# Three places moved in the order of work of a two-block transformer kernel: layer 0's decay, the heads' exponentials, the turned forget gate

## The chip, the cores and the metric

The kernel runs on one core of a Trainium2 chip. The core has a matmul engine (TensorE, PE in the rows; its weight loads are PEld), two engines for elementwise work (VectorE, DVE, and ScalarE, ACT), GpSimd (POOL, idle here), and SyncE (SP), which issues every transfer. The engines run side by side and meet at semaphores. The metric is the time of one execution on the device in microseconds (us), as the median of several runs.

## The reference, cut to what matters

256 tokens of width 1024 pass through two layers of a first block and one layer of a second block, all in float32.

```
first block, twice:
  u = rms_norm(x) @ w_in[l]          -> q, k, v, gates, rank-16 vector rb, memory query qm
  log_a = log_sigmoid(rb @ w_gate_up[l] + b_gate_up[l]) / 16          # "decay"
  oa = softmax attention, 8 heads of 64, causal, ALiBi ("moba")
  ob = gated linear attention, 4 heads, decays log_a ("gla")
  mk, mv = split(rms_norm(mem) @ w_mem_kv[l]); om = softmax(qm mk^T) mv, 4 heads ("mem")
  x  = x + concat(oa, ob, om, each gated) @ w_out[l]
second block, once:
  fg = lb + (1 - lb) * sigmoid(f);  k = 1 - fg;  logf = log(fg)        # "forget"
  o_a = linear attention with k and logf, 8 heads of 128 ("hg")
  o_b = causal softmax attention with low-rank q and kv, 8 heads ("mla")
  x  = x + (sigmoid(gate_a) * (o_a @ w_a) + sigmoid(gate_b) * (o_b @ w_b)) @ w_out
  x  = x + mixture of 64 experts, top group, top 2 in it (SwiGLU, width 512)
  out = rms_norm(x)
```

## The kernel before

**Pieces.** Every projection of the two blocks is cut along its 1024 inputs into eight pieces of 128 rows, most of them 512 columns wide. A piece of weights is first *split* into two fp32r numbers: ScalarE writes the high part `w_hi` (line 1604, a copy), VectorE the low part `w_lo` (line 2010, or 2018 where a gain is folded in). TensorE then does the *mult* of the piece, six matmuls of 512 columns (lines 1116 and 1119): high by high, high by low, low by high, for each of the two tiles of 128 tokens. There are six places for split pieces, and the split of a piece is recorded five pieces ahead of its mult.

**The order is written out by a planner.** `order_of_work` makes one list of steps (`mult`, `split`, `scores`, `exp`, `turn k`, ...), and every engine carries out its own share of each step in this one order. A step whose share on an engine waits holds up all that stands behind it on that engine. Between the pieces stand the steps of the attentions. Two things place them: generators (`attention`, `gla`, `hgrn`) that are advanced by a turn every second piece or so, and `after(n, fn)`, which calls `fn` when n more pieces have been recorded (`tick`, called after each mult). `chain` strings several such calls together.

**The steps that the change touches.** The name of a step is given with its lines in the profile.

- *decay*: TensorE multiplies `rbT` by the gate's weights (line 1159), which VectorE has copied out of the bank as part of *gb out* (line 2007). VectorE adds the bias (2018), ScalarE does Abs, Exp and Ln (*decay log*, line 1601), VectorE ends it. The result is first used by *gla decay*, more than fifteen pieces later. Both 2 KB scratch buffers `sq` are held from *decay* to *decay end*; the next that needs them is *heads sq* of the memory's keys, whose chain goes on by *heads sum*, *heads root*, *heads norm* to *turn k*, transposes on TensorE (line 1099).
- *scores*, *exp*, *turn p*, *values* of a head: TensorE makes the scores (line 1176 for the memory heads, 1183 for moba), VectorE takes the row maxima (2021; for moba and mla it first adds the mask), ScalarE the exponentials (1601), TensorE transposes them (1099), ScalarE copies them back (1604), TensorE multiplies by the values (1215), VectorE scales (2018). A memory head's scores stay in their PSUM bank until its exponential has read them. In each layer the scores of memory heads 1, 2 and 3 all go to one bank (ps3 in layer 0, ps1 in layer 1), before and after the change.
- *forget*, *forget log*, *turn f*: after the sigmoid on ScalarE, VectorE makes fg and k for a tile of tokens (2010 twice, 2015), ScalarE the logarithm (1601), TensorE transposes k (1099, four 128x128), ScalarE copies it (1604). The transposed k is first read when the hg units of that half start, more than ten pieces later.
- *hg scale* on VectorE (2010) and *hg products* on TensorE (1357 and 1359) for a head of the linear attention.

**The experts.** After the mixers come 64 experts of three 2 MB matrices each, in 9 slots. SyncE issues a load as soon as the slot's last reader is through. The first of these loads waits until all engines have passed the end of the gates stage, the next seven for pieces of the last projections.

Of the kernel before, what the change touches and what calls it, by code (L numbers as in the profile page):

```python
# [131 lines left out]
class Plan:  # L132
# [7 lines left out]
    def add(self, *step):  # L140
        self.steps.append(step)
# [6 lines left out]
    def put(self, *banks):  # L148
        self.pool.extend(b for b, _ in banks)
# [49 lines left out]
def order_of_work(uses):  # L199
    P = Plan()  # L200
    add, get, put = P.add, P.get, P.put
# [19 lines left out]
    def after(n, fn):  # L221

        later.append([n, fn])

    def chain(*parts):

        def go(i):
            if i < len(parts):
                def one():
                    if parts[i][1]() is False:  # L230
                        return False
                    go(i + 1)

                after(parts[i][0], one)

        go(0)
# [85 lines left out]

    def attention(a, n):

        for i in range(n + 3):
            while len(P.pool) < 2:
                yield
            if 2 <= i < n + 2:
                B = get()
                add("turn p", a, i - 2, B)  # L330
                put(B)
            if i >= 3:
                B = get()
                add("values", a, i - 3, B)
                put(B)
                done.add((a, i - 3))
            if i < n:
                B = get()
                add("scores", a, i, B)
                P.scores[a, i] = B  # L340
                put(B)
            if 1 <= i < n + 1:
                add("exp", a, i - 1)
            yield

    def stats(n, first=1):
# [88 lines left out]
    def layer(l):  # L435
# [3 lines left out]
        def projections():  # L439
# [4 lines left out]
            for q in ORDER[l]:  # L444
                bs = []
                if q == "gb":
# [9 lines left out]
                        put(B)  # L456
                        chain((1, step("decay log", l, sq)), (1, step("decay end", l, sq, buffers=sq)))

                    after(2, decay)
                elif q == "qkv":  # L460
                    yield from mult(("h", l), [(None, 0, 128, 0, 0), (None, 128, 128, 0, 256), (0, 256, 256, 1, 0),
                                               (1, 256, 256, 1, 256)], bs, there)
# [92 lines left out]
    def group(half):  # L555
# [3 lines left out]
        sq, nt = [P.take("sq") for _ in range(2)], {}  # L559
        add("f out", half, bs, sq)  # L560
        put(*bs)
        for t in range(2):
            def forget(t=t):
                if not P.left("nt"):
                    return False
                nt[t] = P.take("nt")
                add("forget", half, t, sq[t], nt[t])

            def turned(t=t):
                B = get()  # L570
                add("turn f", half, t, nt[t], B)
                put(B)
                P.give(nt[t])
                done.add(("kTd", half, t))

            chain((1 + t, forget), (1, step("forget log", half, t, sq[t], buffers=[sq[t]])), (1, turned))
        yield
        bs = []
        yield from mult(("h", 2), PAIR, bs, there)
# [2327 lines left out]
```

How the kernel before makes its waits and increments, by code:

```python
    def wait_ge(self, sem, value):  # L106
        if sem is not None and self.met.get(sem.name, 0) < value:
            self.met[sem.name] = value
            self.e.wait_ge(sem, value)
# [979 lines left out]
        def tensor(e):  # L1089
# [2 lines left out]
            def room(B):  # L1092
                b, n = B
                w.wait_ge(*ever("outA", b, n - 1))
                w.wait_ge(*ever("outV", b, n - 1))
# [1 line left out]
            def turns(B, src, n, names):  # L1097
                for j in range(n):
                    i = e.transpose(ps(B)[:, j * 128:j * 128 + 128], src[:, j * 128:j * 128 + 128], ident)
                i.then_inc(mark(pe_turn, ("in", *B), *names), 1)
            for kind, *s in plan.steps:
                if kind == "mult":
                    q, lhs, k, jobs, first, final = s
                    hi, lo, ready = operand(lhs, k)
                    wh, wl = RW[q % NRW]
                    w.wait_ge(*at("lo", q))
                    w.wait_ge(*at(*ready))
                    for j, (t, c0, n, B, o) in enumerate(jobs):
                        if first and o == 0:
# [11 lines left out]
                        if names:  # L1122
                            i.then_inc(mark(pe_mult, *names), 1)
                elif kind == "turn":
                    n, k2, B = s
                    src = turned(n, k2)[0]
                    w.wait_ge(s_id, 16)
                    if n == 0:
                        w.wait_ge(s_x[k2 // 4], 16)
                    elif n == "mem":
                        w.wait_ge(s_mem, 16)
                    elif n in (1, 2):
```

## Time and profile before

| | us |
|---|---|
| median of 3 runs | 1625.37 |
| lowest, highest | 1623.73, 1626.02 |
| the profiled execution | 1626.19 |
| its span | 1624.2 |
| TensorE busy | 1470.4 |
| VectorE busy | 621.1 |
| ScalarE busy | 502.9 |

Around the span lie 2.0 us (1626.19 less 1624.2). The span falls in two parts. Up to about 680 us the core does the mixers: TensorE is busy nearly all the time, the transfers about a third of it. From 700 us the experts run and the 16 DMA engines are busy without a break, at about 427 GB/s. Busy time of TensorE is to be read with care, since matmuls overlap and their ends are modelled: the start of the next matmul tells more than the end of the last. The clock that is granted to TensorE is the column PEclk of the tables by window, 1.00 for 2.4 GHz and 0.50 for 1.2 GHz.

### The profile page before, as it was taken

The page shows a single profiled execution, that of the slowest core. Times are in us where ns is not written, and L with a number is a line of the kernel's source. Part 1 is how long each engine was busy: PE and PEld are TensorE (multiplying, and loading weights), DVE is VectorE, ACT ScalarE, POOL GpSimd, SP SyncE. Part 2 cuts the span into 40 slices and gives each one's busy share as a digit, 9 for nine tenths or more (in the row PEclk, how much of TensorE's full clock was granted, in tenths as well). Part 3 has the DMA queues.
Part 4 walks back from the last instruction along what each step waited for, and adds up shares of the span by engine and source line. Part 5 has one row for each costly group of instructions (what it writes and reads, how often), then busy time and mean ns, then how long its engine had stood idle before and what let it go on. Part 6 is the DMA issues. An engine that isn't in the chain of part 4 may idle for free.

```text
span 1624.2 us, 22403 instructions
## 1 busy us (share of the span) xinstructions
PE 1470.4 (91%) x9481; PEld 895.7 (55%) x9481; DVE 621.1 (38%) x1368; ACT 502.9 (31%) x1086; POOL 0.2 (0%) x4
## 2 busy tenths in 40 slices
PE   7999999989999999899999888888888889888886
PEld 6867787778786788744444433343333434433332
DVE  5766666665745657632211211111112111211112
ACT  6666665665645665311111100110011001010102
POOL 0000000000000000000000000000000000000000
PEclk9999999999999999999999999999999999999999
DMA  7422352424324247899999999999999999999995
GB/s 271 165 104 104 108 186 85 155 104 133 124 82 156 85 175 253 353 408 426 427 426 428 427 427 427 428 427 427 426 429 426 427 427 428 427 427 427 428 426 210
DMA packets 72682, 496.53 MB, mean 306 GB/s; under 512 B 6240, under 2 KB 10624, under 8 KB 47616
## 3 DMA queue, kind: packets, MB, share of 16 engines
q1 hardware_dynamic: 72576, 495.03, 74.6%
q8 instruction: 77, 1.26, 0.3%
q14 instruction: 29, 0.24, 0.0%
HBM read 493.96 MB, written 1.05 MB: 305 GB/s over the span
## 4 chain that ended last, share of the span: by engine, by line
PE 43%; DMA 42%; DVE 8%; ACT 5%; issue 1%; SPq 0%; DVEq 0%; ACTq 0%
DMA arena<-in_expert_w 42%; PE ps L1119 18%; PE ps L1465 5%; PE ps L1472 3%; DVE arena L2010 3%; PE ps L1116 2%; PE ps L1486 2%; DVE w_lo L2010 2%; PE ps L1497 2%; ACT arena L1601 2%; ACT arena L1604 1%; ACT w_hi L1604 1%; PE ps L1215 1%; PE ps L1447 1%; DMA arena<-in_w_mem_kv 1%
## 5 line engine op out<-in xcount | busy, mean ns | idle before, releaser
L1465 PE MATMUL ps<-arena 128*32 128x512 f32 x2048 | 250.0, 607 | 94.6 <-DMA arena<-in_expert_w 94.6
L2007 DVE COPY arena<-ps 128x512 f32<-128x512 f32 (+2 forms) x203 | 114.9, 589 | 514.3 <-PE ps L1465 415.4
L1604 ACT ACTIVATE arena<-ps 128x512 f32<-128x512 f32 (+5 forms) x244 | 121.5, 500 | 548.5 <-PE ps L1486 285.7
L1472 PE MATMUL ps<-arena 128*128 128x512 f32 x512 | 255.3, 622 | 0.0
L2010 DVE TENSOR_TENSOR w_lo<-arena,w_hi 128x512 fp32r<-128x512 f32 (+2 forms) x304 | 200.5, 672 | 140.6 <-ACT w_hi L1604 139.4
L1604 ACT ACTIVATE w_hi<-arena 128x512 fp32r<-128x512 f32 (+2 forms) x320 | 194.0, 621 | 111.0 <-PE ps L1119 97.2
L1465 PEld LDWEIGHTS ps<-arena 128*32 128x32 f32 x2048 | 55.7, 110 | 239.1 <-DMA arena<-in_expert_w 150.4
L1119 PE MATMUL ps<-w_hi,hT_hi 128*128 128x512 f32 (+3 forms) x448 | 178.8, 399 | 4.9 <-ACT arena L1601 2.1
L1497 PEld LDWEIGHTS ps<-arena 128*128 128x128 f32 x1024 | 130.0, 192 | 86.1 <-issue 84.1
L1119 PE MATMUL ps<-w_hi,hT_lo 128*128 128x512 f32 (+3 forms) x448 | 168.8, 377 | 0.0
L1119 PE MATMUL ps<-w_lo,hT_hi 128*128 128x512 f32 (+3 forms) x448 | 168.3, 376 | 0.0
L1601 ACT ACTIVATE arena<-ps 128x128 f32<-128x128 f32 (+2 forms) x140 | 48.6, 372 | 340.6 <-PE ps L1497 319.5
L1472 PEld LDWEIGHTS ps<-arena 128*128 128x128 f32 x512 | 88.3, 192 | 118.3 <-issue 117.5
L1497 PE MATMUL ps<-arena 128*128 128x32 f32 x1024 | 132.3, 273 | 0.8 <-DVE arena L2007 0.5
L1486 PE MATMUL ps<-arena 128*32 128x512 f32 x1024 | 123.9, 601 | 0.4 <-DVE arena L2010 0.4
L2010 DVE TENSOR_TENSOR arena<-arena,ps 128x128 f32<-128x128 f32 (+1 forms) x84 | 32.9, 399 | 195.1 <-PE ps L1497 186.6
L1119 PEld LDWEIGHTS ps<-w_hi,hT_hi 128*128 128x128 f32 x448 | 85.8, 192 | 28.9 <-issue 9.5
L1119 PEld LDWEIGHTS ps<-w_hi,hT_lo 128*128 128x128 f32 x448 | 85.9, 192 | 15.0
L1119 PEld LDWEIGHTS ps<-w_lo,hT_hi 128*128 128x128 f32 x448 | 86.2, 192 | 12.8 <-issue 1.2
L2010 DVE TENSOR_TENSOR arena<-arena 128x512 f32<-128x512 f32 (+7 forms) x191 | 73.9, 405 | 13.1 <-ACT arena L1601 7.8
L1601 ACT ACTIVATE arena<-arena 128x128 f32<-128x128 f32 (+7 forms) x132 | 52.2, 399 | 74.4 <-DVE arena L2010 40.7
L1447 PE MATMUL ps<-OH,arena 128*128 128x256 f32 x224 | 62.3, 400 | 3.6 <-DVE arena L2007 3.6
(154 smaller groups left out, 1378.4 us busy)
## 6 DMA issues: line engine op xcount, KB each, us to landing
arena<-in_expert_w SPq DMA_DIRECT2D x191, 2048.0 KB, 41.5
arena<-in_w_in SPq DMA_DIRECT2D x24, 2048.0 KB, 7.8
arena<-in_w_out SPq DMA_DIRECT2D x6, 2048.0 KB, 7.9
arena<-in_w_mem_kv SPq DMA_DIRECT2D x2, 2048.0 KB, 11.9
arena<-in_w_branch_hgrn SPq DMA_DIRECT2D x2, 2048.0 KB, 7.7
arena<-in_w_branch_mla SPq DMA_DIRECT2D x2, 2048.0 KB, 7.8
arena<-in_w_in SPq DMA_DIRECT2D x2, 1536.0 KB, 6.5
arena<-in_mla_w_uq SPq DMA_DIRECT2D x2, 1152.0 KB, 5.5
```

The source lines that it names most:

```text
L1116: i = e.matmul(ps(B)[:, o:o + 256], wp[:, 0, c0:c0 + 128], hp, start=st, stop=en, skip_group_check=True)
L1119: i = e.matmul(ps(B)[:, o:o + n], hp[:, t * 128:t * 128 + 128], wp[:, 0, c0:c0 + n], start=st, stop=en, skip_group_check=True)
L1215: o = e.matmul(ps(B)[:, j * dv:j * dv + dv], T[:, c0 + kt * 128:c0 + kt * 128 + 128], val[:, kt, i * dv:i * dv + dv], start=kt == 0, stop= ...
L1447: i = e.matmul(B, xk[:, t, ks], hot.bitcast(F32), start=t == 0, stop=t == 1)
L1465: o = e.matmul(B[32 * j:32 * j + 32, :], Xs[:, k, q:q + 32], Wn[:, k, :], start=i == 0, stop=i == 1)
L1472: i = e.matmul(acc[t][h][:, :], CT[ex % 2][:, t * 128:t * 128 + 128], Ys[:, h * 512:h * 512 + 512], start=ex == 0, stop=ex == NE - 1)
L1486: i = e.matmul(B[32 * j:32 * j + 32, :], hid[ex % 2][:, 32 * j:32 * j + 32], W2[:, j, h * 512:h * 512 + 512], start=True, stop=True)
L1497: i = e.matmul(B6[:, 128 * h + 32 * j:128 * h + 32 * j + 32], (H1s, H3s)[h][:, j * 128:j * 128 + 128], c("S4"), start=True, stop=True)
L1601: return e.activation(o, i, f, scale=scale, **more)
L1604: return e.activation(o, i, ACTF.Copy, scale=scale)
L2007: return e.tensor_copy(o, i)
L2010: return e.tensor_tensor(o, a, b, op)
```

## The change

It moves steps in the planner's list; no instruction is added or dropped, and there are 31 loads of a function table on ScalarE in either program.

```diff
     def attention(a, n):
 
+        through = set()
+
+        def exp(i):
+            if i not in through:
+                through.add(i)
+                add("exp", a, i)
+
...
                 add("scores", a, i, B)
                 P.scores[a, i] = B
                 put(B)
+                after(1, lambda i=i: exp(i))
             if 1 <= i < n + 1:
-                add("exp", a, i - 1)
+                exp(i - 1)
             yield
...
-                    after(2, decay)
+                    after(5 if l == 0 else 2, decay)
...
-            chain((1 + t, forget), (1, step("forget log", half, t, sq[t], buffers=[sq[t]])), (1, turned))
+            chain((1 + t, forget), (1, step("forget log", half, t, sq[t], buffers=[sq[t]])), (3, turned))
```

1. Layer 0's *decay* stands after mult 12 instead of mult 9; its log and its end move with it.
2. The exponentials of head i stand behind the first mult after its scores, not behind the scores of head i + 1. The code is the same for all three softmax attentions, so it holds for the 8 memory heads of both layers, the 16 moba heads and the 8 mla heads.
3. *turn f* stands two mults later, for each of the two halves.

**ScalarE, memory heads 0 to 3 of layer 0.** `ps,arena 128x256 x2` is one head's exponential, `w_hi` a split, `128x16 x2` is *heads root* of the queries, `ps 128x512` alone the copy of turned exponentials, and `16x4x16` with the two rows behind it *gla collect*. Before:

```order
L1604 ACTIVATE w_hi_63<-arena 128x512
L1604 ACTIVATE w_hi_53<-arena 128x512
L1601 ACTIVATE arena<-arena 128x16 x2
L1601 ACTIVATE arena<-ps,arena 128x256 x2
L1604 ACTIVATE w_hi_55<-arena 128x512
L1604 ACTIVATE w_hi_57<-arena 128x512
L1604 ACTIVATE arena<-ps 128x512
L1601 ACTIVATE arena<-ps,arena 128x256 x2
L1604 ACTIVATE arena<-ps 16x4x16 x4
```

The same place of the changed kernel, whose line numbers are 8 higher:

```order
L1612 ACTIVATE w_hi_63<-arena 128x512
L1609 ACTIVATE arena<-ps,arena 128x256 x2
L1612 ACTIVATE w_hi_53<-arena 128x512
L1609 ACTIVATE arena<-arena 128x16 x2
L1612 ACTIVATE w_hi_55<-arena 128x512
L1609 ACTIVATE arena<-ps,arena 128x256 x2
L1612 ACTIVATE w_hi_57<-arena 128x512
L1612 ACTIVATE arena<-ps 128x512
L1612 ACTIVATE arena<-ps 16x4x16 x4
```

Head 0's exponential now stands ahead of a split and of *heads root*; head 1's ahead of a split and of the copy of head 0's turned exponentials. Further on, head 2's stands behind one split after *gla collect* instead of behind two splits and two copies.

**ScalarE, layer 0's decay log.** It is the row `arena<-arena 128x256 x3`; the row with the table load and the one behind it are *stats root* of the memory rows. Before:

```order
L1596 ACT_TABLE_LOAD
L1601 ACTIVATE arena<-arena 128x2 x2
L1604 ACTIVATE w_hi_57<-arena 128x512
L1604 ACTIVATE w_hi_59<-arena 128x512
L1601 ACTIVATE arena<-arena 128x256 x3
L1604 ACTIVATE w_hi_61<-arena 128x512
```

And in the changed kernel, up to *heads sq* of the memory's keys (the last two rows):

```order
L1604 ACT_TABLE_LOAD
L1609 ACTIVATE arena<-arena 128x2 x2
L1612 ACTIVATE w_hi_57<-arena 128x512
L1612 ACTIVATE w_hi_59<-arena 128x512
L1612 ACTIVATE w_hi_61<-arena 128x512
L1612 ACTIVATE w_hi_63<-arena 128x512
L1612 ACTIVATE w_hi_53<-arena 128x512
L1609 ACTIVATE arena<-arena 128x256 x3
L1612 ACTIVATE w_hi_55<-arena 128x512
L1612 ACTIVATE w_hi_57<-arena 128x512
L1612 ACTIVATE arena<-ps,arena 128x256 x2
L1609 ACTIVATE arena<-ps 128x256 x2
```

Three splits that stood behind the decay log now stand ahead of it, and two splits are left between it and *heads sq*.

**TensorE, the second half's turn f.** `arena 128x128 x4` is one *turn f*, `arena 128x128` alone the first matmul of *hg products* of the fourth head of that unit. Before, from the end of mult 211:

```order
L1119 MATMUL ps<-w_hi_55,hT_lo 128x512
L1099 MATMUL ps<-arena 128x128 x4
L1357 MATMUL ps<-arena 128x128
L1359 MATMUL ps<-arena 16x16 x4
L1359 MATMUL ps<-arena 32x32 x2
L1359 MATMUL ps<-arena 64x64
```

In the changed kernel, from the end of mult 211 to the first *turn f*, with mult 212 between:

```order
L1127 MATMUL ps<-w_hi_55,hT_lo 128x512
L1365 MATMUL ps<-arena 128x128
L1367 MATMUL ps<-arena 16x16 x4
L1367 MATMUL ps<-arena 32x32 x2
L1367 MATMUL ps<-arena 64x64
L1127 MATMUL ps<-w_hi_57,hT_hi 128x512
...
L1107 MATMUL ps<-arena 128x128 x4
```

The products no longer have the two *turn f* ahead of them (the other stood ahead of mult 211).

## Rows read from the trace of the kernel before

**Rows 1.** Page, part 1: busy time of the engines, share of the span, instructions.
```profile
PE 1470.4 (91%) x9481; PEld 895.7 (55%) x9481; DVE 621.1 (38%) x1368; ACT 502.9 (31%) x1086; POOL 0.2 (0%) x4
```

**Rows 2.** Page, part 4: the chain that ended last, by engine.
```profile
PE 43%; DMA 42%; DVE 8%; ACT 5%; issue 1%; SPq 0%; DVEq 0%; ACTq 0%
```

**Rows 3.** Windows: stretch, length, busy us (instructions) by engine, PEclk, DMA share, GB/s.
```profile
500.00:600.00 100.00, 99.07 (x480) 75.75 (x479) 56.94 (x123) 61.54 (x129) 0.00 (x0) 1.00 0.36 127
...
700.00:800.00 100.00, 97.08 (x713) 44.04 (x715) 22.48 (x50) 11.50 (x23) 0.00 (x0) 0.98 1.01 428
```

**Rows 4.** Timeline of SyncE: start, length, issues of expert loads.
```profile
644.44 83.79 SPq L2755 DMA_DIRECT2D arena<-in_expert_w  x17
```

**Rows 5.** Waits of TensorE, 0 to 620 us: total us, times, longest.
```profile
PE ps L1176 <- ACT arena L1601: 5.4, 4, 1.6
...
PE ps L1119 <- ACT arena L1601: 2.1, 3, 1.5
```

**Rows 6.** Windows around TensorE's stops, columns as in Rows 3.
```profile
29.80:36.00 6.20, 6.20 (x16) 4.91 (x17) 4.00 (x12) 4.51 (x9) 0.00 (x0) 0.50 0.08 8
...
114.00:117.60 3.60, 3.60 (x9) 2.24 (x10) 1.32 (x2) 1.11 (x2) 0.00 (x0) 0.58 0.00 0
...
362.30:367.00 4.70, 4.65 (x18) 3.56 (x19) 3.61 (x6) 3.46 (x7) 0.00 (x0) 0.65 0.15 21
...
431.00:435.00 4.00, 3.77 (x11) 3.00 (x11) 2.11 (x5) 3.84 (x7) 0.00 (x0) 0.63 0.00 0
...
133.00:142.00 9.00, 8.12 (x39) 5.89 (x39) 6.44 (x16) 6.44 (x16) 0.00 (x0) 1.00 0.35 144
```

**Rows 7.** Timeline: start, length, instruction, [idle before <-releaser]; decay (PE), split 14 (ACT).
```profile
29.78 1.22 PE L1159 MATMUL ps<-arena 16*128 16x128 f32 x4 [3.10 <-DVE arena L2007]
...
31.07 0.70 ACT L1604 ACTIVATE w_hi<-arena 128x512 fp32r<-128x512 f32 x1
```

**Rows 8.** Waits of ScalarE from 33 to 46 us.
```profile
ACT w_hi L1604 <- PE ps L1119: 3.1, 4, 1.2
```

**Rows 9.** Timeline: memory keys' root (ACT), norm (DVE), first turn k (PE).
```profile
45.43 0.46 ACT L1601 ACTIVATE arena<-arena 128x8 f32<-128x8 f32 x2 [1.40 <-DVE arena L2015]
...
48.01 0.76 DVE L2010 TENSOR_TENSOR arena<-ps,arena 128x256 f32<-128x256 f32 x2
...
49.76 0.38 PE L1099 MATMUL ps<-arena 128*128 128x128 f32 x2
```

**Rows 10.** Timeline of TensorE: scores of memory heads 2 and 3, layer 0.
```profile
104.94 1.13 PE L1176 MATMUL ps<-arena 64*128 64x256 f32 x4 [1.60 <-ACT arena L1601]
...
112.78 1.13 PE L1176 MATMUL ps<-arena 64*128 64x256 f32 x4 [1.11 <-ACT arena L1601]
```

**Rows 11.** Timeline of VectorE: maxima of head 1; gla collect's share.
```profile
101.46 0.69 DVE L2021 TENSOR_REDUCE arena<-ps 128x2 f32<-128x512 f32 x1
...
107.10 0.68 DVE L2010 TENSOR_TENSOR arena<-ps,arena 128x512 f32<-128x512 f32 x1
```

**Rows 12.** Timeline of ScalarE: head 1's exponential; gla collect; a moba split.
```profile
103.87 0.47 ACT L1601 ACTIVATE arena<-ps,arena 128x256 f32<-128x256 f32 x1
...
107.88 1.85 ACT L1604 ACTIVATE arena<-ps 16x64 f32<-16x64 f32 x7 [2.99 <-DVE arena L2010]
...
151.82 0.63 ACT L1604 ACTIVATE w_hi<-arena 128x512 fp32r<-128x512 f32 x1 [1.17 <-PE ps L1119]
```

**Rows 13.** Timeline: TensorE's first turn f, VectorE's second forget, first half.
```profile
362.35 0.66 PE L1099 MATMUL ps<-arena 128*128 128x128 f32 x4 [2.95 <-DVE arena L2015]
...
364.26 0.43 DVE L2015 TENSOR_SCALAR arena<-arena 128x512 f32<-128x512 f32 x1
```

**Rows 14.** Timeline, second half: VectorE's hg scale; TensorE's second turn f and products.
```profile
439.17 1.29 DVE L2010 TENSOR_TENSOR arena<-arena 128x512 f32<-128x512 f32 x2
...
439.31 0.66 PE L1099 MATMUL ps<-arena 128*128 128x128 f32 x4
440.61 0.46 PE L1357 MATMUL ps<-arena 128*128 128x128 f32 x2 [0.64 <-DVE arena L2010]
```

## The prediction, as it was put on record before the changed kernel ran

> **What bounds the kernel now.** I read the page first. TensorE is busy for 91% of the span [rows 1]. The chain that ended last is 43% TensorE and 42% transfers [rows 2]. The two do not compete for the same stretch: from 500 to 600 us TensorE is busy 99.07 of 100 us while the DMA share is 0.36, and from 700 to 800 us the DMA share is 1.01 at 428 GB/s [rows 3]. So the mixers are TensorE's and the experts are the transfers'. What joins them is the issue of expert loads: it starts at 644.44, and every load waits for TensorE or VectorE to free its slot [rows 4]. Behind that point nothing is changed. Each microsecond by which the mixers' last stage comes earlier should therefore shift the whole expert part rigidly, and each microsecond that TensorE does not lose before 640 us is one off the time. A step that is merely moved beside busy matmuls is worth nothing; what counts is where TensorE stops.
>
> I took the waits of TensorE next, then the windows around each stop. The memory heads' scores wait 5.4 us for exponentials, in four places [rows 5]. The first decay matmul waits 3.10 us [rows 7], the first turn f 2.95 us [rows 13]. A stop has a second price: after some of them the clock falls to 0.50 for a few us. The windows show means of 0.50, 0.58, 0.65 and 0.63 [rows 6]. What that costs is the stretch times one less the clock: 6.20 x 0.50 = 3.1 us behind the decay, 3.60 x 0.42 = 1.5 us behind memory head 3 (layer 1 has the same two stops and the same fall, so four score waits are two pairs), 4.70 x 0.35 = 1.6 us behind turn f, and 4.00 x 0.37 = 1.5 us at 431, behind a wait of 1.5 us that the change doesn't touch [rows 5]. But from 133 to 142 us the clock stays at 1.00 although TensorE is busy for only 8.12 of 9 us [rows 6]. A stop of about 1 us alone need not bring a fall.
>
> **Part 1, layer 0's decay.** Before, TensorE is through with mult 9 at 26.7 and stands until 29.78 for VectorE's copy of rb [rows 7]. Behind the move it goes straight into mults 10, 11 and 12, whose split pieces are ready, and comes to the decay at about 30.6, when the copy is done. So the wait of 3.10 and the slow stretch of 3.1 go: 6.2 us. What is late next? ScalarE. It is held by a table load and a root until 31.07 [rows 7] and then has to make the splits that TensorE uses from 32.6 on (mult 14). At 0.70 us on ScalarE [rows 7] and about as much on VectorE for a split, each low part is ready within 0.1 us of its mult up to mult 15. The decay log's three instructions (1.3 us), which used to run while TensorE crawled, now stand two splits ahead of heads sq of the memory's keys and wait for VectorE's z until about 36.1. The chain from heads sq to the first turn k is fixed in length. ScalarE waited 3.1 us for TensorE between 33 and 46 us [rows 8], and that slack is used up, but no more: I put heads root at 42.65 instead of 45.43 and the first normed half at 48.4 - 2.8 = 45.6 instead of 48.4 (the first of the two in the row at 48.01) [rows 9]. TensorE without its stop and at full clock would be at that turn k at 49.76 - 6.2 = 43.6. So a new stop of 2.0 us takes its place, and the net gain is 4.2 us. The bounds: 6.2 if ScalarE keeps up, and 2.2 if it comes 2 us later still. The new stop may bring a fall of the clock of its own; of 1.6 us I count half, +0.8. Nothing else needs the decay early, and it issues no DMA; SyncE's next weight load hangs on mult 15's low part, which comes a little earlier than before.
>
> **Part 2, the exponentials.** The scores of memory head 2 wait for the bank of head 1, which head 1's exponential frees [rows 10]. Its maxima are ready at 101.46 + 0.69 = 102.15 [rows 11], but ScalarE first did two splits and a copy and began it at 103.87 [rows 12]. Moved ahead of one split and the copy, it can run at 102.2 and be done at 103.1. TensorE has the transposes ahead of it until 103.34, so the whole 1.60 goes. Head 3's scores wait for head 2's exponential. That one stands behind gla collect, and ScalarE's part of gla collect cannot begin before VectorE's share at 107.10 + 0.68 is done [rows 11]. VectorE works without a gap up to there, so this does not come earlier. ScalarE ends gla collect at 109.7 [rows 12], makes one split, and is done with the exponential (0.9 us) at 111.2; before, the scores behind it started at 112.78. TensorE is itself 1.6 us earlier there, so its wait of 1.11 stays [rows 10]. The second stop is kept, the first goes. The price of the clock behind them, 1.5 us, is kept or goes with it: half, 0.8. Mult 56's first matmul also waits about 0.3 us for head 3's exponential, which the new order frees (the two short ones of the three waits in [rows 5] are this one in both layers). Per layer 1.6 + 0.8 + 0.3 = 2.7, for two layers 5.4. Bounds for one layer: 1.6 (clock falls all the same, short wait stays) and 3.4.
>
> The other 24 heads: only one moba head of layer 0 makes TensorE wait, 0.3 us. In exchange ScalarE now stands at each exponential until VectorE has the maxima, with a split queued behind it, and VectorE and TensorE wait for that split. What covers this is the lead of the splits: in the moba stage ScalarE itself waits for TensorE, 1.17 us before the split at 151.82 [rows 12], so a split is ready five mults, 5 x 1.37 = 6.8 us, ahead of its use. A wait of about 1 us is hidden. I take -0.3 in all.
>
> **Part 3, turn f.** First half: TensorE waits 2.95 us for VectorE, then crawls [rows 13]. Now it does two mults of 1.37 us each first (six matmuls at 0.23), from 359.3, and arrives at 362.0; the first k is ready at 362.3, a wait of 0.3. The second is ready at 364.26 + 0.43 = 364.7 [rows 13] and TensorE arrives one turn f and one mult later, at 364.1, a wait of 0.6. Gain 2.95 - 0.9 + 1.6 for the clock = 3.7 us (2.0 to 4.6). Second half: there hg products wait until 440.61 for VectorE's hg scale, which runs from 439.17 to 440.46 [rows 14]. VectorE sets this, not TensorE. Before, the two turn f lay inside that wait for nothing. TensorE came to the one at 439.31 at about 439.0, with another (0.4 us) behind it one mult earlier. Now the products come first, at 438.6, wait 2.0 us in place of 0.64 and some 0.3 at the turn f, start at 440.61 as before, and the two turn f are paid behind them: 2 x 0.4 = +0.8 us. A fall of the clock may come with the longer stop: +0.4. This part alone is a loss.
>
> **The sum.** -4.2 + 0.8 - 5.4 - 0.3 - 3.7 + 0.8 + 0.4 = -11.6 us against the profiled execution's 1626.19, whose span is 1624.2 with 2.0 us around it: 1614.6. The median of the runs shown, 1625.37, lies 0.8 lower, so I forecast 1613.8.
>
> **Rivals.** (a) *The clock falls wherever there is a stop.* It then falls at the new stop (+0.8 more), in both layers behind head 3 (+1.6), and at the products (+0.4): -11.6 + 2.8 = -8.8, 1616.6. For it: two stops of 1.60 and 1.11 do bring a fall. Against it: 133 to 142 us [rows 6]. The Trainium skill, "TensorE: Matmul & The Clock Gate", section "A second HAM failure mode: psum-queue depth-cycling", says that frequent short idle gaps between groups of matmuls can swing the clock between its two levels; by that this rival holds, and the trace bears it out at 114 us but not at 133.
>
> (b) *The clock is spared everywhere*, since no stop above 2 us is left: -0.8 - 1.6 - 0.4 more, -14.4, 1611.0. Against it: the fall at 431 comes behind 1.5 us.
>
> (c) *The decay only moves its stop.* If ScalarE, loaded with the table load, roots and splits, reaches the memory keys' root at its old time, part 1 gives 6.2 - 4.8 = 1.4 instead of 3.4 (4.2 less 0.8): 1615.8; with (a) on top 1618.6. For it: VectorE and ScalarE were 60% busy in that stage. Against it: the 3.1 us of slack.
>
> (d) *The gain is hidden by the transfers.* If the expert loads' rate and not their start set the end, the time stays at 1625.4. For it: DMA share 1.01 from 700 us on. Against it: a full pipe that starts earlier ends earlier, and its first load waits for an engine [rows 4].
>
> (e) *Slower: exponentials hold the splits.* Place: ScalarE in the moba and mla stages, 24 heads. If the wait for the maxima were not covered by the lead, each head would cost about 1 us of TensorE, +24 for -11.6, 1637; with half of them, 1625 to 1626. It decides from the point where ScalarE has less than about 1 us of its own waits per head, since then the lead shrinks head by head. The 1.17 us at 151.82 lie just above this; the mla stage, busy 99.07 of 100 us, has no visible stop to gain either.
>
> **Chances.** Forecast 0.44, (a) 0.20, (b) 0.13, (c) 0.10, (d) 0.07, (e) 0.06. A measurement of this kernel can tell 0.2%, 3.3 us, from no change. The forecast and (a) to (c) are all faster by more than that: 0.87. Of (d) and (e) I give 0.08 to no difference and 0.05 to slower. The range goes beyond (b) by the upper ends of the bounds and beyond (a) with (c) by a little: 1606.5 to 1620.5. It leaves (d) and (e) outside.
>
> **What would show it.** Right: L1167 (the decay) without an idle gap; the first turn k of the memory's keys at about 45.6 with an idle gap of about 2 us before it; memory head 2's scores without a wait and head 3's with about 1.1 us, in both layers; no stop above 0.7 us at the first half's turn f; a stop of about 2 us at L1365 in the second half; the first expert load about 11.6 us earlier, with an expert part as long as before. Wrong: an expert part that is longer or shorter by more than a us or two; gaps of TensorE before w_lo in the moba and mla stages; a clock below 1.00 in windows that have no counterpart above.

## The result, and the profile after

The changed kernel ran in 1614.19 us (median of 4 runs, 1613.9 to 1616.18) against 1625.14 us for the kernel before (4 runs, 1623.73 to 1626.02). The ratio is 0.9936, with a 95% interval from 0.9924 to 0.9947: faster by 11 us, forecast 11.6. The profiled execution took 1613.9 us, its span is 1612.0 us, 12.2 us shorter than before. In the changed kernel's trace all line numbers of the code behind the edit are 8 higher.

The page first, busy time and the chain by engine:

```profile
PE 1469.1 (91%) x9481; PEld 895.4 (56%) x9481; DVE 620.3 (38%) x1368; ACT 501.4 (31%) x1086; POOL 0.2 (0%) x4
...
DMA 43%; PE 42%; DVE 8%; ACT 5%; issue 1%; SPq 0%; DVEq 0%; ACTq 0%
```

The instruction counts are those of [rows 1] (ScalarE loads a function table 29 times in either trace, not the 31 times given with the change), and the busy time is within 1.5 us of it, so nothing was saved by doing less. The chain has shifted from TensorE to transfers by a point [rows 2]. SyncE's expert loads in the timeline (start, length):

```profile
631.99 122.64 SPq L2763 DMA_DIRECT2D arena<-in_expert_w  x26
```

They begin 12.45 us earlier than in [rows 4]. From there to the end of the span are 980.0 us, before 979.8. The expert part moved as a block, and what has to be explained lies before 632 us.

TensorE's waits from 0 to 620 us (total us, times, longest), against [rows 5]:

```profile
PE ps L1184 <- ACT arena L1609: 2.4, 2, 1.2
...
PE ps L1365 <- DVE arena L2018: 1.8, 1, 1.8
...
PE ps L1280 <- DVE arena L2022: 1.7, 1, 1.7
PE ps L1127 <- ACT arena L1609: 1.5, 1, 1.5
...
PE ps L1107 <- DVE arena L2018: 1.0, 1, 1.0
...
PE ps L1107 <- DVE arena L2023: 0.6, 2, 0.3
```

Of the score waits two of four are left, and of the three mult waits for an exponential (2.1 us) only the long one: both short ones are gone. The first turn k (L1107 behind L2018) waits anew, and the products (L1365) wait 1.8 us in place of 0.64 [rows 14]. The timeline of TensorE at the places of the forecast, with the idle gap before each in brackets:

```profile
31.38 0.48 PE L1167 MATMUL ps<-arena 16*128 16x128 f32 x2
...
45.52 0.44 PE L1107 MATMUL ps<-arena 128*128 128x128 f32 x2 [0.96 <-DVE arena L2018]
...
107.01 0.70 PE L1184 MATMUL ps<-arena 64*128 64x256 f32 x2 [1.22 <-ACT arena L1609]
...
253.44 0.91 PE L1184 MATMUL ps<-arena 64*128 64x256 f32 x3 [1.21 <-ACT arena L1609]
...
350.40 0.66 PE L1107 MATMUL ps<-arena 128*128 128x128 f32 x4 [0.23 <-DVE arena L2023]
...
352.79 0.66 PE L1107 MATMUL ps<-arena 128*128 128x128 f32 x4 [0.34 <-DVE arena L2023]
...
359.36 0.71 PE L1280 MATMUL ps<-arena 128*128 128x128 f32 x4 [1.72 <-DVE arena L2022]
...
425.56 0.46 PE L1365 MATMUL ps<-arena 128*128 128x128 f32 x2 [1.79 <-DVE arena L2018]
```

The decay has no gap, where it had 3.10 [rows 7]. The first turn k starts at 45.52. Head 3's scores keep a gap of 1.2 in both layers, and head 2's have none [rows 10]. The first half's turn f has two short gaps in place of 2.95 [rows 13]. The spread of the rows (L1280) is a place that the forecast did not name. In the kernel before it reads:

```profile
374.40 0.71 PE L1272 MATMUL ps<-arena 128*128 128x128 f32 x4 [0.99 <-DVE arena L2014]
```

Its gap grew by 0.7 us. The windows of the changed kernel (columns as in Rows 3; PEclk stands ahead of the DMA share):

```profile
26.00:31.00 5.00, 5.00 (x24) 4.14 (x23) 4.20 (x9) 4.91 (x9) 0.00 (x0) 1.00 0.25 93
105.00:113.00 8.00, 6.78 (x38) 5.17 (x36) 3.22 (x7) 6.59 (x18) 0.00 (x0) 1.00 0.22 84
252.00:258.00 6.00, 4.79 (x23) 3.36 (x22) 3.23 (x7) 4.59 (x11) 0.00 (x0) 1.00 0.21 76
350.00:364.00 14.00, 11.71 (x78) 10.22 (x78) 9.42 (x17) 9.01 (x17) 0.00 (x0) 1.00 0.35 114
412.00:420.00 8.00, 6.41 (x33) 4.45 (x32) 4.83 (x12) 6.62 (x11) 0.00 (x0) 0.79 0.01 2
422.00:432.00 10.00, 8.21 (x45) 6.35 (x44) 6.44 (x11) 3.83 (x9) 0.00 (x0) 0.83 0.39 118
```

Against [rows 6], the clock is at 1.00 at the first four places, still falls behind the old wait of 1.5 us (412 to 420), and falls at a new place, behind the products' stop (10 x 0.17 = 1.7 us).

To see where the gain arises I subtract the start of the same matmul in two traces. The lead of a kernel over the kernel before, in us, at the start of some mults (numbered as in the order of work):

| kernel | first turn k (22) | behind memory heads, layer 0 (57) | behind moba (76) | layer 1 (129) | behind first turn f (172) | behind spread (177) | behind products (214) |
|---|---|---|---|---|---|---|---|
| changed | 4.2 | 7.9 | 8.1 | 11.8 | 16.9 | 15.0 | 12.6 |
| changed, again (e8) | 4.3 | 6.4 | 6.6 | 8.7 | 13.7 | 11.9 | 9.5 |
| e1 decay alone | 4.2 | 4.5 | 4.5 | 4.8 | 4.5 | 4.8 | 4.9 |
| e2 exponentials alone | 1.6 | 5.4 | 5.6 | 9.3 | 9.8 | 10.5 | 10.6 |
| e3 turn f alone | 0.2 | 0.5 | 0.5 | 0.5 | 5.4 | 3.6 | 1.2 |
| e4 turn f, first half only | 3.9 | 6.0 | 6.3 | 10.0 | 15.0 | 13.2 | 13.2 |
| e7 later collection | 4.2 | 8.3 | 8.6 | 12.7 | 17.7 | 18.2 | 17.2 |

In e7 the spread itself stands two mults later, so 18.2 is still ahead of it; behind it the lead is 17.2.

### The profile page after: what moved, and what is told of

Read it like the earlier page. It is cut to its first block, busy times and chain, and to the rows that moved or that the text cites. A ratio compares the mean times of both kernels' runs of the same rounds, so it can differ in the third digit from the quotient of the medians.

```text
span 1612.0 us, 22419 instructions
## 1 busy us (share of the span) xinstructions
PE 1469.1 (91%) x9481; PEld 895.4 (56%) x9481; DVE 620.3 (38%) x1368; ACT 501.4 (31%) x1086; POOL 0.2 (0%) x4
## 4 chain that ended last, share of the span: by engine, by line
DMA 43%; PE 42%; DVE 8%; ACT 5%; issue 1%; SPq 0%; DVEq 0%; ACTq 0%
DMA arena<-in_expert_w 42%; PE ps L1127 16%; PE ps L1473 5%; PE ps L1480 4%; DVE arena L2018 3%; PE ps L1124 2%; PE ps L1494 2%; DVE w_lo L2018 2%; PE ps L1505 2%; ACT w_hi L1612 2%; ACT arena L1609 2%; ACT arena L1612 1%; PE ps L1223 1%; PE ps L1455 1%; DMA arena<-in_w_mem_kv 1%
## 5 line engine op out<-in xcount | busy, mean ns | idle before, releaser
L2018 DVE TENSOR_TENSOR w_lo<-arena,w_hi 128x512 fp32r<-128x512 f32 (+2 forms) x304 | 200.7, 673 | 146.9 <-ACT w_hi L1612 146.3
L2018 DVE TENSOR_TENSOR arena<-arena,ps 128x128 f32<-128x128 f32 (+1 forms) x84 | 32.9, 398 | 196.7 <-PE ps L1505 188.2
L1609 ACT ACTIVATE arena<-arena 128x256 f32<-128x256 f32 (+7 forms) x132 | 52.4, 399 | 101.0 <-DVE arena L2018 41.0
L2018 DVE TENSOR_TENSOR arena<-arena 128x512 f32<-128x512 f32 (+7 forms) x191 | 73.9, 405 | 13.1 <-ACT arena L1609 7.9
## 6 DMA issues: line engine op xcount, KB each, us to landing
arena<-in_w_mem_kv SPq DMA_DIRECT2D x2, 2048.0 KB, 12.2
```

Source lines behind the costliest of these rows:

```text
L1609: return e.activation(o, i, f, scale=scale, **more)
L2018: return e.tensor_tensor(o, a, b, op)
```

## The experiments

The kernel before was run beside each group. It took 1625.16 us (19 runs) beside e1 to e4, 1625.79 us (7 runs) beside e5 to e8, and 1625.23 us (7 runs) beside e9 to e11.

### e1: the decay alone

```
-                    after(2, decay)
+                    after(5 if l == 0 else 2, decay)
```

> Only layer 0's decay is moved (to behind mult 12); exponentials and turn f stand as before. Theory (the moves act one by one, each by the stop of TensorE at its place): mult 22 starts 4.2 us earlier than before, with a stop of about 1 us at the first turn k of the memory's keys as in the changed kernel; behind that the lead stays at 4.2, so the time is 4.2 lower, 1621 against 1625.1. The stops of 1.6 and 1.1 us at the memory heads 2 and 3 are there in both layers. Rival (the falls of the clock depend on when a stop happens as much as on how long it is): with everything 4.2 us earlier, some of the falls behind head 3, behind turn f and at 431 us are gone or others are there, each worth about 1.6 us, so that the lead changes by that at places where no instruction was moved.

Measured: 1621.3 us (10 runs), ratio 0.9975 (0.9966 to 0.9985). The lead is 4.2 us from mult 22 on and stays between 4.5 and 4.9. TensorE's first turn k in its trace:

```profile
45.47 0.44 PE L1099 MATMUL ps<-arena 128*128 128x128 f32 x2 [1.63 <-DVE arena L2010]
```

The move removes its stop and its slow stretch and gets back a stop of 1.6 us: 4 us net, as expected. Rival (c), 1.4, is out. Head 2's stops of 1.6 us are there in both layers; head 3's are 0.9 and not 1.1. The clock still falls once at the memory heads of each layer, but in layer 0 already behind head 2's stop (100 to 108 us; the kernel before has 1.00 in this stretch and falls behind head 3):

```profile
100.00:108.00 8.00, 7.31 (x31) 5.31 (x32) 4.86 (x11) 3.73 (x14) 0.00 (x0) 0.79 0.75 263
```

### e2: the exponentials alone

```
+                after(1, lambda i=i: exp(i))
             if 1 <= i < n + 1:
-                add("exp", a, i - 1)
+                exp(i - 1)
```

> Only the exponentials stand one mult behind their scores; decay and turn f as before. Theory: in each layer the stop of 1.6 us at head 2 goes, that of head 3 stays at 1.2, and no fall of the clock follows it, because one stop there is left of two: a lead of 3.7 us per layer, 7.4 in all plus 0.3 for the moba head, time 1617.4. Rival (the changed kernel was spared the fall only because the decay's move had shifted these places by 4.2 us): the clock falls behind head 3 in at least one layer, the lead is 2.2 there, time 1619 to 1620.5. Second rival (what the changed kernel gained here came from the decay's move): under 2 us per layer.

Measured: 1616.97 us (4 runs), ratio 0.9952 (0.9935 to 0.9969). The lead grows by 3.7 us over layer 0's memory heads and by about as much in layer 1. Its waits of TensorE from 60 to 300 us and its window over layer 0's memory heads:

```profile
PE ps L1184 <- ACT arena L1609: 2.4, 2, 1.2
```
```profile
104.00:113.00 9.00, 7.79 (x41) 5.98 (x40) 4.75 (x11) 5.88 (x17) 0.00 (x0) 1.00 0.60 225
```

Head 2's stop is gone, head 3's stands, the clock did not fall behind it in this execution. The time is within 0.5 us of the expected 1617.4. Some of this trace's lead is not the change's: 1.6 us at mult 22 lie ahead of anything that was moved, since the decay's stop was followed by a shorter slow stretch than before, and 1.1 us come at the first half's turn f, which was not moved either. Its stop is the 2.95 us of [rows 13], but here the clock did not fall behind it:

```profile
352.92 0.66 PE L1107 MATMUL ps<-arena 128*128 128x128 f32 x4 [2.96 <-DVE arena L2023]
```
```profile
350.00:360.00 10.00, 6.74 (x33) 5.39 (x34) 7.89 (x13) 7.13 (x12) 0.00 (x0) 1.00 0.30 95
```

### e3: turn f alone, in both halves

```
-... (1, turned))
+... (3, turned))
```

> Only turn f is moved two mults on, in both halves. Theory: the first half gives 3.2 to 3.7 us, the second half loses 0.8 by the two transposes that are paid behind the products, and 1.6 more if the clock falls at the longer stop there: time lower by 0.8 to 2.9, 1622.2 to 1624.3. Rival (the second half loses nothing of its own, and the loss of 2.4 us seen between mults 210 and 214 belongs to the other moves): lower by 3.2 or more, 1622 or less.

Measured: 1625.01 us (10 runs), ratio 0.9999 (0.999 to 1.0009): no difference, below the expected 0.8 to 2.9, though the interval does not exclude its lower end. The lead says why it is so small: +4.9 at the first turn f, then -1.8 at the spread, then -2.4 at the products, 0.7 in all. Waits of TensorE from 350 to 445 us, and two windows:

```profile
PE ps L1357 <- DVE arena L2010: 1.8, 1, 1.8
PE ps L1272 <- DVE arena L2014: 1.7, 1, 1.7
```
```profile
360.00:372.00 12.00, 9.71 (x56) 7.79 (x55) 9.04 (x17) 8.57 (x16) 0.00 (x0) 1.00 0.41 132
427.00:443.00 16.00, 13.54 (x71) 10.46 (x72) 10.54 (x19) 8.70 (x15) 0.00 (x0) 0.79 0.25 74
```

From 427 to 443 us the clock is at 0.79, while the same stretch of the kernel before has 0.89: another slow stretch, behind the products' new stop.

### e4: turn f in the first half only

The whole change, except:

```
-... (3, turned))
+... (1 if half else 3, turned))
```

> The changed kernel with turn f moved in the first half alone; in the second it stands as before. Theory: products again start with a stop of about 0.6 us behind the turn f, the clock does not fall there, and the lead at mult 214 is 15 us instead of 12.6: 2.4 us less than the changed kernel, 1611.8. If the clock falls there for another reason (the stop of 1.5 us at mult 208 is near), 0.8 us less, 1613.4. Rival (the products are late whatever stands ahead of them, so the order doesn't matter): no difference, 1614.2.

Measured: 1612.88 us (4 runs), ratio 0.9926 (0.991 to 0.9943). The lead of 13.2 at the spread is kept through the products, where the changed kernel loses 2.4. The times alone would not show this: the two kernels' ratios have overlapping intervals (e9 against e11, below, does show it). TensorE's wait there is a short one, and the window behind it is at full clock:

```profile
PE ps L1365 <- DVE arena L2018: 0.6, 1, 0.6
```
```profile
107.00:113.00 6.00, 5.73 (x18) 3.73 (x19) 2.56 (x7) 2.99 (x8) 0.00 (x0) 0.72 0.01 4
...
425.00:434.00 9.00, 8.28 (x51) 6.36 (x50) 6.65 (x12) 5.14 (x9) 0.00 (x0) 1.00 0.44 131
```

The upper row is a surprise. Up to there the order of work is the changed kernel's, and so is the stop, yet here the clock fell behind it (6 x 0.28 = 1.7 us). That fits the time, 1.1 us above the expected 1611.8, and the lead, 13.2 and not 15. Hence e8.

### e5: early exponentials for the memory heads alone

```
-                after(1, lambda i=i: exp(i))
+                if a[0] == "mem":
+                    after(1, lambda i=i: exp(i))
```

> The whole change, but the exponential moves up behind its scores for the memory heads alone; the 24 heads of the moba and mla stages keep theirs one pass later. My account (only the memory heads' stops are worth something there): the time of the whole change plus at most 0.5 us, 1614.2 to 1614.7, and the lead over the kernel before is flat from mult 57 to mult 125 in layer 0 up to the one moba head's 0.3 us. Rival 1 (the exponentials hold the splits, but only a little, so that it was hidden in the sum): one or more us faster than the whole change, 1613 or less. Rival 2 (the 24 heads' exponentials are worth more than the 0.3 us I gave them): 1615.5 or more.

Measured: 1616.79 us (4 runs, 1613.98 to 1619.24), ratio 0.9945 (0.9928 to 0.9962). Beside the changed kernel on the same chip (e8, 1617.13 us) that is no difference. The single runs scatter too widely to place it against the limits of 0.5 and 1 us, so the time is inconclusive. The lead is clearer: from mult 57 to 76 the changed kernel gains 0.2 us in both of its traces and this one 0.03. The 24 other heads' exponentials are worth the 0.2 to 0.3 us of one moba head and cost nothing: rival (e) is out.

### e6: the spread of the rows two mults later

e4, and besides (this line runs in the first half only; the text below says both halves by mistake):

```
-            after(1, spread)
+            after(3, spread)
```

> The whole change, but with the turned forget gate moved only in the first half, and with the spread of the rows behind it two mults later (3 in place of 1 in both halves). In the changed kernel TensorE stops 1.7 us at the first half's spread, 0.7 more than before. If that stop is a true loss, it goes, and this runs 1.7 us below the version that moves only the first half's gate (1612.9): 1611.2. Rival 1: the spread's later result makes the scaled keys late, and the stop comes back at the products: 1612.9, same time, with the stop elsewhere. Rival 2: the clock falls at a stop that it was spared, +1.5: 1612.7 to 1614.4.

Measured: 1612.38 us (4 runs), ratio 0.9919 (0.9902 to 0.9936). The spread's gap, 1.72 in the changed kernel:

```profile
362.67 0.60 PE L1280 MATMUL ps<-arena 128*128 128x128 f32 x3 [0.40 <-DVE arena L2022]
```

Its first expert load starts at 629.80, e4's at 631.28: 1.5 us earlier, as expected, with the same clock fall in layer 0 in both. The lead shows where: over the second turn f and the spread it falls by 0.5 (15.1 to 14.6), in e4 by 1.8 (15.0 to 13.2). The clock did not fall behind the wait at mult 208 in this trace as it did in e4's, but that is not in the gain: the lead rises by 1.5 there and is back at 14.6 behind the second half's turn f, where TensorE waits for VectorE. e4 ran in another group, the medians differ by 0.5 us only, inside both intervals, and the spans by 0.3 (1610.5 and 1610.8), since the expert part was 1.1 us longer in e6. So the trace shows the gain up to the first expert load, the times do not.

### e7: the collection of the gla stage one pass later

e6, and besides, ahead of `add("gla collect", ...)`:

```
+            if t == 1:
+                yield
```

> As the version with the later spread, and the collection of the gla stage one pass later, so that memory head 2's exponential stands ahead of it on ScalarE. Head 3's scores waited 1.2 us for that exponential in each layer. By my account (the exponential stood behind the collection, which waited for VectorE) both stops go: 2 x 1.2 = 2.4 us below that version, 1608.8 if it runs at 1611.2, and another 1.5 for each fall of the clock behind head 3 in it. Rival 1: the collection's own readers come late and TensorE stops there instead, no gain. Rival 2: head 3's stop stays since its exponential waits for VectorE's maxima, no gain either, with the stop still at the scores.

Measured: 1608.94 us (4 runs, 1608.24 to 1609.53), ratio 0.9897 (0.988 to 0.9914), on the same chip 3.4 us below e6. No wait for an exponential is left at the scores. TensorE's waits from 60 to 300 us that take their place, and the windows:

```profile
PE ps L1263 <- ACT arena L1611: 1.2, 2, 0.6
```
```profile
105.00:113.00 8.00, 7.40 (x43) 5.82 (x41) 3.17 (x8) 5.39 (x17) 0.00 (x0) 1.00 0.23 86
252.00:259.00 7.00, 6.39 (x35) 4.87 (x34) 2.69 (x6) 4.67 (x16) 0.00 (x0) 1.00 0.11 39
```

Two stops of 1.2 us went and two of 0.6 came (2 x 0.6 = 1.2 us), the clock fall in layer 0 (1.5 to 1.7) went too. The leads of the two traces differ by 2.6 (17.2 and 14.6), and the rest of the 3.4 is within the scatter. So the account holds, and half of what rival 1 says as well: one half of each stop came back at the next place. It is the fastest version of the study.

### e8: the changed kernel once more

> The changed kernel once more, unchanged. Its time: 1614.2 again within 1 us. What it tells apart is the clock: in the first look no fall came behind memory head 3's stop of 1.2 us in layer 0, yet one came behind the same stop, with the same instructions up to there, in the version that differs only in the second half of the turned gate. If the instructions fix the clock, the falls are the same as in the first look of this kernel (417 and 427 us). If the clock's answer to a stop of about 1 us varies between executions, they differ, and the lead over the kernel before at mult 57 differs by about 1.5 us.

Measured: 1617.13 us (4 runs, 1614.73 to 1618.27), ratio 0.9944 (0.9928 to 0.9961). The time is 2.9 us above the expected 1614.2, where 1 us was allowed; the clock says why. The windows of the first trace, then this one's:

```profile
108.00:112.50 4.50, 4.50 (x22) 3.34 (x22) 2.04 (x6) 3.10 (x9) 0.00 (x0) 1.00 0.00 0
255.00:259.50 4.50, 4.50 (x27) 3.62 (x25) 1.50 (x4) 3.14 (x9) 0.00 (x0) 1.00 0.00 0
```
```profile
108.00:112.50 4.50, 4.50 (x14) 3.30 (x14) 1.96 (x6) 1.56 (x3) 0.00 (x0) 0.62 0.00 0
255.00:259.50 4.50, 4.50 (x10) 2.54 (x11) 1.84 (x5) 2.56 (x5) 0.00 (x0) 0.62 0.02 4
```

It is the same program with the same stop of 1.22 us at 107 us, and TensorE runs at full clock behind it in one execution and at 0.62 in the other. Each fall costs 4.5 x 0.38 = 1.7 us, and the lead at mult 57 is lower by 1.5, at mult 129 by 3.1. The two traces may come from different chips, which would be a rival. e6 excludes it for layer 1: it ran on the chip of e8, its order of work is the same up to the spread at 360 us, and its stop at head 3 of layer 1 is the same 1.20 us, yet the clock stayed:

```profile
255.00:259.50 4.50, 4.30 (x19) 3.05 (x19) 2.53 (x6) 3.10 (x8) 0.00 (x0) 1.00 0.02 5
```

The clock's answer to such a stop varies from execution to execution.

### e9 to e11: one part taken back from e7, and e7 again

e9 moves turn f in the second half too, e10 puts the decay back, e11 is e7 unchanged:

```
-... (1 if half else 3, turned))
+... (3, turned))                        # e9
-                    after(5 if l == 0 else 2, decay)
+                    after(2, decay)      # e10
```

> The version with the later collection, and the turned gate moved in the second half too. My account: the two turn f (0.8 us) are paid behind the products, and the clock falls behind the products' stop of 1.8 us (1.6 more), as in the three traces that have both: 2.4 us above the version with the later collection on the same chip. Rival 1: the clock is spared, 0.8 above. Rival 2: the products come earlier than I think and the move is free, 0.

> The version with the later collection, and the decay of layer 0 back at its old place. My account: 4.2 us above the version with the later collection (6.2 of stop and slow clock come back, 2.0 of the stop at the memory keys go), plus at most 1.5 if the clock then falls at one more place. Rival: the decay's own stop was only moved, 1.4 above.

> The version with the later collection once more, unchanged, beside the two that take one part of it back: 1608.9 within 1 us. No stop of its memory heads is above 1.1 us, so no fall of the clock before 640 us, as in its first look, and a spread of its single runs below 2 us where the changed kernel's was 3.5. If the falls come by chance at any stop, this trace has one or two of them before 640 us and the single runs scatter as widely as the changed kernel's.

Measured, 4 runs each: e9 1613.1 us, ratio 0.992 (0.9904 to 0.9937); e10 1612.77 us, 0.9922 (0.9905 to 0.9938); e11 1609.59 us (1609.39 to 1609.82), 0.9903 (0.9887 to 0.992). The products in e9 and then in e11, and the window behind them, e9's first:

```profile
423.40 0.77 PE L1367 MATMUL ps<-arena 128*128 128x128 f32 x2 [3.39 <-DVE arena L2020]
```
```profile
423.68 0.46 PE L1367 MATMUL ps<-arena 128*128 128x128 f32 x2 [0.64 <-DVE arena L2020]
```
```profile
423.00:432.00 9.00, 8.60 (x42) 6.93 (x43) 3.35 (x6) 2.51 (x5) 0.00 (x0) 0.64 0.44 131
```
```profile
423.00:432.00 9.00, 8.36 (x57) 7.14 (x57) 5.62 (x9) 5.71 (x14) 0.00 (x0) 1.00 0.42 131
```

The products start when VectorE lets them, at 423.4 and at 423.7 (the two traces lie 0.3 us apart from the start). Moving turn f behind them only turns work into a stop: 0.8 us for the two turn f and 9 x 0.36 = 3.2 us of slow clock, 3.5 us in the times. (The window begins 0.4 us before the products, so a little of the slow stretch lies in the stop.) The direction was right and the expected 2.4 too small: in e9 the clock had not fallen behind the older wait at mult 208, TensorE was at the products 1.6 us earlier for it, and the fixed start turned that into a longer stop, 3.4 us for 1.8, with a longer slow stretch.

e10 against e11 isolates the decay: 3.2 us in the times, expected 4.2. TensorE's decay and the window around it, then e11's window:

```profile
29.65 0.59 PE L1169 MATMUL ps<-arena 16*128 16x128 f32 x3 [3.49 <-DVE arena L2017]
```
```profile
26.00:36.00 10.00, 6.51 (x23) 5.10 (x23) 7.69 (x20) 8.76 (x16) 0.00 (x0) 0.83 0.18 57
```
```profile
26.00:36.00 10.00, 10.00 (x46) 8.02 (x45) 8.31 (x21) 8.32 (x14) 0.00 (x0) 1.00 0.19 60
```

The stop is there, but the slow stretch behind it costs 10 x 0.17 = 1.7 us and not the 3.1 of [rows 6]. That length varies too; e2 had the same 3.49 and 0.83 in this window. Of the 3.2 us, 2.5 are there at mult 22 (leads 1.4 and 3.9).

e11 confirms e7's time. In both traces every stretch of 100 us from 20 to 620 us has PEclk 1.00. Ahead of that e11 has one fall, which its expectation excluded: PEclk is 0.72 from 12 to 18 us, and 1.00 in e7. It costs little in the end, since the start of the first turn k is fixed: the two traces are 1.0 us apart at mult 8 and 0.25 at mult 22.

The four runs of e11 lie within 0.43 us, those of e7 within 1.29, the eight of the changed kernel within 4.37. It would be rash to put that down to head 3's stops. e6 has them, with a fall of the clock in its trace, and its four runs lie within 0.40; e9 is without them and scatters by 2.81. The versions with the long stop at the products all scatter by 2.3 us or more (the changed kernel 2.3 and 3.5, e3 2.4, e5 5.3, e9 2.8), and the others with that stop at 0.6 or less by 2.2 or less, but the kernel before, whose products wait 0.64, has 2.8 over its 19 runs. What makes a version steady is not shown.

## Why the prediction was right, point by point

**The frame.** What TensorE loses before the first expert load is time, the rest moves as a block. In the traces of all thirteen runs the stretch from the first expert load to the end of the span is 979.6 to 981.0 us, while its start moves by 17 us. Rival (d) is out.

**Part 1, -4.2 + 0.8.** The first turn k was put at 45.6 and stands at 45.52, since the chain over ScalarE sets it: heads root was put at 42.65 and is at 42.47.

```profile
42.47 0.46 ACT L1609 ACTIVATE arena<-arena 128x8 f32<-128x8 f32 x2 [1.38 <-DVE arena L2023]
```

In this trace the decay comes at 31.38, not 30.6, but TensorE was 0.7 us behind the kernel before already at mult 8, ahead of anything moved; in e1 and e7 it comes at 30.07 and 30.20. The stop is 1.0 to 1.6 in place of 2.0. That changes nothing in the sum, because the end of the stop is fixed. The half price of 0.8 for a clock fall there was not paid in any of the traces with the move. e10 measured 3.2 for the whole part where the forecast's net term is 3.4, but that they agree is luck: the forecast has the half price for a fall at turn k, which never came, and e10 lost 1.4 us less in its slow stretch than [rows 6] has. Against the slow stretch of the kernel before the part is worth 4.2 (e1 3.9 in the times).

**Part 2, -5.4 - 0.3.** Mechanism right: head 2's stop gone, head 3's kept at 1.2, mult 56's short waits gone. The size in the first trace is 3.7 per layer and not 2.7, because the clock was spared in both layers where half a fall had been counted. A fall was also priced 0.2 too low: the forecast's window from 114.00 to 117.60 [rows 6] ends before the slow stretch does. Up to 119 it costs 5 x 0.34 = 1.7 us, not 1.5:

```profile
114.00:119.00 5.00, 5.00 (x16) 3.50 (x17) 1.32 (x2) 1.70 (x3) 0.00 (x0) 0.66 0.00 0
```

In e8 it fell in both, with gains of 2.1 in layer 0 and 2.1 in layer 1 (8.7 - 6.6). Half a price stood for "falls or not"; over the twelve places (six traces with a stop of 1.2 us at head 3, two layers) the clock fell at five.

The reason given for head 3's stop holds as well. ScalarE's part of gla collect has to wait for VectorE, so it should not come earlier for the 1.6 us that TensorE gains at head 2. It starts at:

```profile
103.69 1.84 ACT L1612 ACTIVATE arena<-ps 16x64 f32<-16x64 f32 x7 [3.67 <-DVE arena L2018]
```

That is 4.2 us earlier than in [rows 12], which is the lead that the decay had given ahead of the memory heads (4.2), and not TensorE's lead behind head 2 (5.9). In e2, where that lead is 1.7, it starts at 106.22, 1.7 us earlier. What the forecast took as given is the order on ScalarE: e7 puts head 2's exponential ahead of the collection, and the stop goes.

**Part 3, first half -3.7.** At mult 172 the gain is 5.0 us, at mult 177 it is 3.2: 1.8 us went at the spread and the second turn f. The spread's rows come from VectorE behind the forget gates, and a TensorE that arrives earlier waits longer there. That stop is the answer to "what is late next" that the forecast left out, and e6 removed 1.3 of the 1.7 us. The forecast's own two waits at turn f were smaller than put, 0.23 and 0.34 for 0.3 and 0.6.

**Part 3, second half +0.8 + 0.4.** Products' stop put at 2.0, measured 1.79, start unchanged, two turn f paid behind it: right. The clock's share is 1.6 instead of 0.4: it fell in all five traces that have the products' stop of 1.8 us or more (changed kernel twice, e3, e5, e9), and in none of those without it. Here half a price was too low. For head 3's stops of 1.2 us, with five falls in twelve, it is about right. The length of a stop does not decide it: the table in the last section has stops of 1.7 us that were never followed by a fall and one of 2.96 us that was spared.

**The sum and the rivals.** With the clock as in the first trace: 4.2 + 7.6 + 3.2 - 2.4 = 12.6 at mult 214, 12.2 in the span. Against the forecast's terms part 1 gave 0.8 more (3.4), part 2 gave 1.9 more (5.7), both by the clock; the first half gave 0.5 less (3.7) by the missed stop and the second half cost 1.2 more (1.2) by the clock. Together that is 1.0 us more, where one term alone is off by 1.9. The time is closer than its terms, and that is luck. Over all 8 runs of the changed kernel the median is 1615.5 us, 1.7 above the forecast and 1.1 below rival (a)'s 1616.6. Of the four places where rival (a) has the clock fall, e8 shows three, all but the first turn k; but as a rule for every stop it is wrong, since the stop of 1.7 us at the spread and the two of 1.5 us for oS_lo were spared even there. At head 3 the forecast's half and rival (a) are two executions of one program, not two theories. The Trainium skill, "TensorE: Matmul & The Clock Gate", section "A second HAM failure mode: psum-queue depth-cycling", tells of a kernel in which frequent short gaps between groups of matmuls make the clock swing between its two levels. The traces agree that it swings, by the 1.00 and 0.62 above, and add that a fall can come behind one stop of 1.2 us, though not in every execution.

## What to carry to other kernels

Follow the chain that releases TensorE, not TensorE's stop: where another engine sets the start (the products), work moved out of the wait gains nothing ahead of it and is paid in full behind it (0.8 us), with a slow stretch on top where the clock falls. Where a stop is removed, walk on to the next instruction that waits for another engine, since an earlier arrival turns up there as a new stop. Before crediting a version with a few us on TensorE's clock, profile it more than once: two traces of the changed kernel, which has stops of 1.2 us, differ by 3 us at the first expert load.

## What the runs showed of the hardware that was not expected

- The granted clock behind one and the same stop of 1.2 us was 1.00 in one execution and 0.62 over 4.5 us in another, with identical instructions. The length of a stop does not tell whether a fall comes. TensorE's stops of 1 us and more from 20 to 620 us in the thirteen traces, with the falls that began in them or behind them:

| stop before | us | places | falls |
|---|---|---|---|
| mults that wait for oS_lo, both layers | 1.50 | 26 | 0 |
| first turn k, decay moved | 0.96 to 1.63 | 9 | 0 |
| spread, turn f moved and the spread not | 1.71 to 1.72 | 5 | 0 |
| second half's turn f, not moved and no fall at mult 208 | 1.03 to 1.07 | 5 | 0 |
| head 3's scores, exponentials moved | 1.19 to 1.23 | 12 | 5 |
| mult 208, in every version | 1.53 to 1.55 | 13 | 6 |
| first half's turn f, not moved | 2.95 to 2.96 | 3 | 2 |
| heads 2 and 3, exponentials not moved (a pair is one place) | 1.60 and 0.9 to 1.1 | 6 | 6 |
| products, with turn f behind them | 1.79 to 3.39 | 5 | 5 |
| decay, not moved | 2.39 to 3.49 | 4 | 4 |

The wait for oS_lo in the changed kernel, and the stretch with one of the two:

```profile
PE ps L1127 <- DVE oS_lo L2018: 3.0, 2, 1.5
```
```profile
120.00:220.00 100.00, 96.70 (x561) 80.41 (x560) 68.62 (x161) 61.98 (x140) 0.00 (x0) 1.00 0.39 138
```

- The slow stretch at the decay's stop varies in length. The mean clock from 26 to 36 us is 0.83 in e2 and e10; in the kernel before it is 0.66:

```profile
26.00:36.00 10.00, 6.91 (x20) 5.16 (x19) 7.70 (x21) 8.26 (x15) 0.00 (x0) 0.66 0.16 48
```

- What stays open: why the stops of the first four rows of the table are always spared when head 3's shorter one often is not. No run varied what TensorE does around them.
